# Two transformer blocks on one core: a token norm fed by a one-hot product, an earlier begin of a scan's operands, and q/k row sums in four row groups

## The chip, the cores and the metric

The kernel runs on one core of a Trainium2 chip. The metric is the device time in microseconds (us) of one execution, as the median of several runs. TensorE multiplies matrices, VectorE (DVE) and ScalarE (ACT) work on elements, GpSimd (POOL) builds masks and does some products, SyncE (SP) issues most of the transfers. Each engine runs its own list of instructions in order, and waits on semaphores for the others.

## The reference, cut to what matters

Two blocks follow one another on the same 1024 tokens of 1024 features. Three places of them matter here. The first is the norm of q and k in the first block's attention, over 64 features for each of 4 heads and 2 halves:

```python
q = rms_norm(q, g_q) * (HEAD_DK ** -0.5)
k = rms_norm(k, g_k)
```

The second is the seam of the blocks. 16 experts each pick 128 tokens (`idx`) and add their gated output to those rows; then the second block begins with a layer norm, whose result `h` feeds a projection and, times `DEEPNORM_ALPHA`, a residual:

```python
return jax.vmap(lambda ib, yb: jnp.zeros((S, D), yb.dtype).at[ib.reshape(-1)].add(yb.reshape(-1, D)))(idx, y)
...
h = layer_norm(x, ln_emb_g, ln_emb_b)
proj = jnp.einsum('bld,de->ble', h, w_in[i])
...
out = jnp.einsum('ble,ed->bld', mix, w_out[i]) + b_out[i]
h = layer_norm(DEEPNORM_ALPHA * h + out, ln1_g[i], ln1_b[i])
```

The third is the chunked scan of the second block: 8 chunks of 128 tokens by 2 groups of heads, which makes 16 steps. Each needs the decays `exp(segment sums)`, the inputs `x * dt`, and the state that the steps before have built.

## The kernel before

The program is seven blocks, one after the other, with a barrier between them. Inside a block the order on every engine is written by hand. Names used below: `Q` is PSUM, eight banks of 512 columns; `arena` is SBUF, cut into tiles of 1024 columns (`tiles(n)`); `W` is a ring of three slots for weight units of 2 MB, which SP refills as soon as the last reader of a slot is done; `hT_high` and `hT_low` are the two parts into which a float32 operand is split for three fast products. A plain float32 product shows in the trace as two records for one instruction, and is said below to be one float32 product.

**The q/k stage** (290.4 to 343.9 us of the trace). ScalarE squares the eight tiles of q and k. TensorE sums them over 64 features: `sums(g)` multiplies each by an 8-column mask into rows 0 to 7 (q) or 64 to 71 (k) of two PSUM banks. ScalarE takes the root (`root`), VectorE the reciprocal (`invert`) of these 8 rows by 1024 columns, `high_rows` and `low_rows` split them, and `spread` multiplies them back to 128 rows, for VectorE to scale q and k (`norm`, 8 of them). Between these, TensorE forms six vectors from weight units (`mod_product`, line 327; `next_vector(i)` is the row product of vector i and then the product of unit i + 1), VectorE adds their biases (`added`) and copies the far parts of the attention bias (lines 1064 and 1065).

**The token norm** (1250.2 to 1308.4 us). When the last expert's product is done, VectorE scales it (`outputs`) into `y_e`, GpSimd scatters it with add onto the tokens in DRAM (`scatter`), SP loads eight tiles of 128 tokens (`xt`), and VectorE normalizes each with two `bn_stats`, an aggregate, a reciprocal and two passes over 1024 columns (lines 2128 and 2130). TensorE turns each tile (8 transposes, line 1938), ScalarE and VectorE split the result (`emb_T`, `low_part`). From the fifth tile on, TensorE puts 12 products of the projection behind each tile. At the end it turns the small vectors (line 1951).

**The scan's begin** (from 1776 us). SP loads the segment sums of each step by broadcast (`send_sums`) into one of three places, `i % 3`, and the x inputs in four pieces (`send_xs`). ScalarE makes the decays (`decays`) and copies B out of PSUM (`read_turned`), VectorE makes `x * dt` (`inputs`) and the masked B C product (`chunk_cb`), GpSimd multiplies the decays by it. TensorE's `chunk(c)` needs both inputs of the chunk before.

## Time and profile before

| | |
|---|---|
| median of 3 runs (lowest, highest) | 2180.46 us (2178.20, 2182.43) |
| the profiled execution: time, span of its trace | 2185.76 us, 2184.0 us |
| mean granted TensorE clock, as a share of 2.4 GHz | 0.966 |
| TensorE busy | 2071.8 us, 95% of the span |
| VectorE busy | 1684.9 us, 77% |
| ScalarE busy | 1066.9 us, 49% |
| GpSimd busy | 215.8 us, 10% |

All times inside the kernel are positions in the one profiled execution, counted from its first instruction. Busy shares are means over stages with different limits, so each stage is read by itself. "Granted clock" 1.00 is TensorE's upper level (2.4 GHz), 0.50 its lower one (1.2 GHz). TensorE counts as busy from its first record to its last in a run of them, also at the lower level.

### The profile page before, as it was taken

How to read it: one execution, taken by the hardware profiler on the slowest of the kernel's cores; microseconds unless marked ns; L12 is line 12 of the kernel's file. 1: busy time of each engine (PE TensorE's matmuls, PEld its weight loads, DVE VectorE, ACT ScalarE, POOL GpSimd, SP SyncE). 2: the span in 40 equal slices, each digit the busy share in tenths (PEclk: the TensorE clock that was granted, in tenths of full speed). 3: DMA queues.
4: the chain of work that ended last, by engine and by line, in shares of the span. 5: the costliest groups of instructions: out<-in, count | busy, mean ns of one | idle time of the engine just before them, and what ended most of it. 6: DMA issues, size and time to landing. Idle time of an engine off the chain costs nothing. (4 is left out here: it accounts for less than half of the span.)

```text
span 2184.0 us, 24904 instructions
## 1 busy us (share of the span) xinstructions
PE 2071.8 (95%) x9840; PEld 1603.5 (73%) x9840; DVE 1684.9 (77%) x1714; ACT 1066.9 (49%) x1217; POOL 215.8 (10%) x168
## 2 busy tenths in 40 slices
PE   6999998999997999999999859999999998999998
PEld 4767844777865788888888647888888874588876
DVE  5575157895557899999999777999999977864776
ACT  4488134894235677777777522112222167523043
POOL 0200010001000011110110100000000013234040
PEclk9999997999988999999999969999999999899999
DMA  8311171003368999999999741111222245333121
GB/s 304 92 39 39 39 261 43 1 1 90 130 264 338 348 382 400 395 391 400 393 401 392 236 164 42 49 68 40 76 78 97 96 142 187 141 140 116 39 78 58
DMA packets 131071, 381.71 MB, mean 175 GB/s; under 512 B 9580, under 2 KB 22156, under 8 KB 130977
## 3 DMA queue, kind: packets, MB, share of 16 engines
q1 hardware_dynamic: 117184, 340.41, 40.9%
q0 software_dynamic: 7568, 23.09, 4.3%
q10 hardware_dynamic: 6224, 16.93, 1.9%
q8 instruction: 63, 1.03, 0.2%
q14 instruction: 32, 0.25, 0.0%
HBM read 337.28 MB, written 43.06 MB: 174 GB/s over the span
## 5 line engine op out<-in xcount | busy, mean ns | idle before, releaser
L2473 DVE SCALAR_TENSOR_TENSOR arena<-arena,vecs 128x1023 f32<-128x1023 f32 (+14 forms) x240 | 304.4, 1268 | 7.1
L2049 DVE TENSOR_TENSOR w_low<-W,w_high 128x2048 fp32r<-128x2048 f32 x96 | 216.9, 2286 | 34.2 <-ACT w_high L1970 34.2
L2049 DVE TENSOR_TENSOR w_low<-arena,w_high 128x2048 fp32r<-128x2048 f32 x96 | 218.4, 2289 | 19.3 <-ACT w_high L1970 19.3
L1822 PE MATMUL Q<-hT_high,w_high 128*128 128x512 f32 (+1 forms) x736 | 230.0, 392 | 1.3 <-PEq L1842 1.3
L1822 PE MATMUL Q<-hT_low,w_high 128*128 128x512 f32 (+1 forms) x720 | 225.0, 390 | 0.0
L1970 ACT ACTIVATE w_high<-arena 128x2048 fp32r<-128x2048 f32 x96 | 184.2, 1919 | 74.1 <-PE Q L1888 74.1
L1822 PE MATMUL Q<-hT_high,ring_low 128*128 128x512 f32 x704 | 219.9, 390 | 0.0
L1970 ACT ACTIVATE w_high<-W 128x2048 fp32r<-128x2048 f32 x96 | 184.0, 1919 | 69.3 <-PE Q L1888 65.6
L1835 ACT ACTIVATE w_high<-W 128x1024 fp32r<-128x1024 f32 x44 | 46.6, 1059 | 256.1 <-PE Q L1822 243.0
L1888 PE MATMUL Q<-w_high,x_high 128*128 128x512 f32 x512 | 160.9, 396 | 2.4 <-DVE x_low L2052 2.4
L1822 PEld LDWEIGHTS Q<-hT_high,w_high 128*128 128x128 f32 (+1 forms) x736 | 135.4, 184 | 33.2 <-issue 1.8
L1888 PE MATMUL Q<-w_low,x_high 128*128 128x512 f32 x512 | 158.9, 392 | 0.0
L1888 PE MATMUL Q<-w_high,x_low 128*128 128x512 f32 x512 | 158.7, 391 | 0.0
L1822 PEld LDWEIGHTS Q<-hT_low,w_high 128*128 128x128 f32 (+1 forms) x720 | 134.1, 186 | 29.6
L1822 PEld LDWEIGHTS Q<-hT_high,ring_low 128*128 128x128 f32 x704 | 132.6, 188 | 27.8
L1888 PEld LDWEIGHTS Q<-w_low,x_high 128*128 128x128 f32 x512 | 97.1, 190 | 20.5
L1888 PEld LDWEIGHTS Q<-w_high,x_high 128*128 128x128 f32 x512 | 95.9, 190 | 21.7 <-DVE x_low L2052 2.8
L1888 PEld LDWEIGHTS Q<-w_high,x_low 128*128 128x128 f32 x512 | 96.8, 189 | 20.4
L468 PE MATMUL Q<-h_high,in_high 128*128 128x512 f32 x254 | 100.7, 396 | 0.0
L469 PE MATMUL Q<-h_high,ring_low 128*128 128x512 f32 x254 | 99.4, 391 | 0.0
L470 PE MATMUL Q<-h_low,in_high 128*128 128x512 f32 x254 | 99.1, 390 | 0.0
L1173 DVE CUSTOM_DVE_ANT_0 arena<-Q,arena 128x1024 f32<-128x1024 f32 x64 | 76.0, 1223 | 22.5 <-PE Q L1128 22.4
(466 smaller groups left out, 4139.9 us busy)
## 6 DMA issues: line engine op xcount, KB each, us to landing
arena<-in_w_dram SPq DMA_DIRECT2D x48, 2048.0 KB, 12.3
W<-in_w_dram SPq DMA_DIRECT2D x48, 2048.0 KB, 13.2
W<-in_w_mod_dram SPq DMA_DIRECT2D x12, 2048.0 KB, 13.3
W<-in_w_in_dram SPq DMA_DIRECT2D x12, 2048.0 KB, 9.2
W<-in_w_out_dram SPq DMA_DIRECT2D x6, 2048.0 KB, 10.8
spill<-arena ACTq DMA_DIRECT2D x24, 512.0 KB, 2.6
W<-in_w_in_dram SPq DMA_DIRECT2D x8, 1024.0 KB, 8.8
arena<-spill SPq DMA_DIRECT2D x3, 2048.0 KB, 10.8
```

Source lines behind the costliest of these rows:

```text
L468: nc.tensor.matmul(bank, w_high, h_high, start=first, stop=False)
L469: nc.tensor.matmul(bank, w_low, h_high, start=False, stop=False)
L470: return nc.tensor.matmul(bank, w_high, h_low, start=False, stop=last)
L1173: nc.vector.tensor_tensor_reduce(out=score[i % 3][j], in0=bank2(j), in1=bias, scale=1.0, scalar=3.0e38, op0=ALU.add, op1=ALU.min, accum_ou ...
L1822: ins = nc.tensor.matmul(Q[rows, 2 * pair_of(n) + half, :], w[:, k], x[:, k, HALF * half:HALF * half + HALF], start=k == 0 and w is high a ...
L1835: nc.scalar.activation(high, src, ACT.Copy).then_inc(split_high, 1)
L1888: ins = nc.tensor.matmul(Q[:, bank + n, :], x[:, kx], w[:, k, HALF * n:HALF * n + HALF], start=kx == 0 and x is high and w is wh, stop=kx ...
L1970: nc.scalar.activation(split_of(r, j)[0][:], chunk_src(r, j), ACT.Copy).then_inc(high_ready, 1)
L2049: nc.vector.tensor_tensor(wl[:], chunk_src(r, j), wh[:].bitcast(F32), ALU.subtract).then_inc(low_v, 1)
L2473: ins = nc.vector.scalar_tensor_tensor(conf[:, i, j:], u[:, 0:S - j], w, conf[:, i, j:], ALU.mult, ALU.add)
```

## The change

Three edits that don't touch one another.

1. **q/k norm.** The mask `qk_sum` repeats its 8 columns to 32, and `sums` computes four blocks of 32 output rows, one for each quarter of the 1024 columns, all in one bank. The rows are now 128 by 256 instead of 8 by 1024 for root, reciprocal and split; a column of 0 and 1 (`lower`, `sign`) makes half of each group of rows carry the low part, and VectorE writes them with four instructions of 32 rows into `qk_parts`. The mask for `spread` is the transpose of `qk_sum`, made on TensorE. The eight spreads and norms move between the other work.
2. **Token norm.** SP loads the first four tiles before the last expert's sums are scattered. TensorE adds them: the tile times the identity, plus a one-hot matrix (`picked`, made on VectorE from `idx`) times `y_e`, both float32. Statistics are read from PSUM. ScalarE does the first pass (scale and shift), VectorE one pass for the gain. The bias `ln_emb_b` is added on TensorE behind each transpose as a one-row product, and for the residual in a row `row_sum` = ALPHA * ln_emb_b + b_out. `turn_vecs` moves ahead of the last tiles' products.
3. **The scan's begin.** The sums' places change to 0, 1, 0, 1, 2, 0, 1, ... (`sums_place`), so that step 2's are asked for in step 3's old place. `read_turned(1)` moves into `decays(2)`, and `inputs(1)` moves ahead of the last three products of `conf` (k = 5, 6, 7).

The diff, cut to its core:

```diff
-        qk_sum = tiles(5)[:, 0:HEADS * VECS].rearrange("p (b r) -> p b r", b=HEADS)
...
+        QUARTER, REPEAT = S // 4, P // VECS
+        qk_sum = tiles(4)[:, 0:HALF].rearrange("p (b r) -> p b r", b=HEADS)
...
+        qk_high = rounded("qk_high", 2, [P, 4, QUARTER])
...
-                        for half in range(2):
-                            ins = nc.tensor.matmul(Q[rows_of(g), sum_bank[g] + half, :], qk_sum[:, b],
-                                                   tiles(n % 2)[:, HALF * half:HALF * half + HALF],
+                        for q in range(4):
+                            ins = nc.tensor.matmul(Q[32 * q:32 * q + 32, sum_bank[g], 0:QUARTER], qk_sum[:, b, 0:32],
+                                                   tiles(n % 2)[:, QUARTER * q:QUARTER * q + QUARTER],
                                                    start=b == 0, stop=b == HEADS - 1)
...
                             next_vector(2 * g + b // 2)
+                        if g and b:
+                            spread(b - 1)
                         if n == 1:
                             near()
...
+                    if g:
+                        spread(HEADS - 1)
+                def spread(n):
+                    g, b = divmod(n, HEADS)
+                    pe.wait_ge(mask_ready, 1)
                     pe.wait_ge(parts_low, g + 1)
...
+                    if n >= 2:
+                        pe.wait_ge(qk_normed, n - 1)
+                    for half in range(2):
+                        ins = nc.tensor.matmul(Q[:, 6 * (n % 2) + half, :], qk_spread[:, b],
+                                               qk_parts[:, HALF * half:HALF * half + HALF], start=True, stop=True)
+                    ins.then_inc(spread_mm, 1)
...
                 def invert(g):
                     dve.wait_ge(root_q, g + 1)
-                    nc.vector.reciprocal(qk_rows[rows_of(g)], qk_rows[rows_of(g)]).then_inc(rows_inv, 1)
+                    nc.vector.reciprocal(qk_rows[:, g], qk_rows[:, g]).then_inc(rows_inv, 1)
+                    dve.wait_ge(rows_inv, g + 1)
+                    nc.vector.tensor_scalar_mul(qk_lower, qk_rows[:, g], lower).then_inc(qk_lower_ready, 1)
                 def low_rows(g):
                     dve.wait_ge(parts_high, g + 1)
-                    nc.vector.tensor_tensor(qk_parts[rest_of(g)], qk_rows[rows_of(g)],
-                                            qk_parts[rows_of(g)].bitcast(F32), ALU.subtract).then_inc(parts_low, 1)
+                    dve.wait_ge(qk_lower_ready, g + 1)
+                    if g:
+                        dve.wait_ge(spread_mm, HEADS)
...
+                    for q in range(4):
+                        at = slice(32 * q, 32 * q + 32)
+                        ins = nc.vector.scalar_tensor_tensor(
+                            qk_parts[at, QUARTER * q:QUARTER * q + QUARTER], qk_high[at, 2 + g].bitcast(F32),
+                            sign[at], qk_lower[at], ALU.mult, ALU.add)
+                    ins.then_inc(parts_low, 1)
...
-                for h in range(HEADS):
+                def far(h):
...
+                far(0)
+                for n in range(HEADS - 1):
+                    norm(n)
+                    far(n + 1)
                 added(3)
+                norm(HEADS - 1)
                 invert(1)
+                low_rows(1)
                 added(4)
-                norm(0)
-                low_rows(1)
-                for n in range(1, HEADS):
-                    norm(n)
+                norm(HEADS)
+                norm(HEADS + 1)
                 added(5)
-                for n in range(HEADS, 2 * HEADS):
-                    norm(n)
+                norm(HEADS + 2)
+                norm(HEADS + 3)
...
+        sums_place = [i if i < 2 else (i - 2) % 3 for i in range(STEPS)]
+        def sums_of(i):
+            return cs_bc[sums_place[i]]
...
         def send_sums(sync, i):
...
-            sync.dma_start(cs_bc[i % 3], rows.broadcast_to((P, HPG * P))).then_inc(cs_in[i % 3], 16)
+            sync.dma_start(sums_of(i), rows.broadcast_to((P, HPG * P))).then_inc(sums_in(i)[0], 16)
...
+                sync.wait_ge(*low_level(E, 3))
+                sync.dma_start(b_row, A["ln_emb_b_2"].rearrange("(o n) -> o n", o=1)).then_inc(rows_b_in, 16)
+                sync.dma_start(bo_row, A["b_out_2"][0].rearrange("(o n) -> o n", o=1)).then_inc(rows_b_in, 16)
+                sync.wait_ge(h_tr, E)
+                sync.wait_ge(y_added, 16 * (E - 1))
+                for t in range(PICKED):
+                    sync.dma_start(xt[t], tokens_acc[P * t:P * t + P]).then_inc(xt_in[t], 16)
+                sync.wait_ge(row_sum_ready, 1)
+                sync.dma_start(row_sum, b_sum).then_inc(row_stored, 16)
+                sync.wait_ge(emb_sum, PICKED)
                 sync.wait_ge(y_added, 16 * E)
-                for t in range(NT):
+                for t in range(PICKED, NT):
                     sync.dma_start(xt[t], tokens_acc[P * t:P * t + P]).then_inc(xt_in[t], 16)
                 for t in range(NT):
...
+                def token_sum(t):
+                    pe.wait_ge(xt_in[t], 16)
+                    if t >= 2:
+                        pe.wait_ge(emb_scaled, t - 1)
+                    for n in range(2):
+                        nc.tensor.matmul(Q[:, 4 + 2 * (t % 2) + n, :], ident[:], xt[t][:, HALF * n:HALF * n + HALF],
+                                         start=True, stop=False)
+                    if t == 0:
+                        pe.wait_ge(picked_ready, 1)
+                        pe.wait_ge(y_ready, E)
+                    for n in range(2):
+                        ins = nc.tensor.matmul(Q[:, 4 + 2 * (t % 2) + n, :], picked[:, t],
+                                               y_e[:, HALF * n:HALF * n + HALF], start=False, stop=True)
+                    ins.then_inc(emb_sum, 1)
+                def turn_vecs():
+                    pe.wait_ge(small2_in, 16 * (4 + NT + 8))
...
+                    ins.then_inc(vec_tr, 1)
+                pe.wait_ge(y_ready, E - 1)
+                token_sum(0)
+                pe.wait_ge(rows_b_in, 32)
                 for t in range(NT):
+                    if t + 1 < PICKED:
+                        token_sum(t + 1)
                     pe.wait_ge(emb_ready, t + 1)
                     if t >= 2:
                         pe.wait_ge(emb_T_low, t - 1)
                     for k in range(KD):
...
+                        turned_k = Q[:, 2 * (t % 2) + k // 4, P * (k % 4):P * (k % 4) + P]
+                        nc.tensor.matmul(turned_k, xt[t][:, P * k:P * k + P], ident[:], start=True, stop=False,
+                                         is_transpose=True)
+                        ins = nc.tensor.matmul(turned_k, b_row[:, P * k:P * k + P], ones[0:1, :],
+                                               start=False, stop=True)
                     ins.then_inc(emb_tr, 1)
+                    if t == NT - 2:
+                        turn_vecs()
...
-                root(0)
-                for t in range(NT):
-                    if t + 1 < NT:
-                        root(t + 1)
+                def emb_high(t):
                     act.wait_ge(emb_tr, t + 1)
...
+                root(0)
+                for t in range(NT):
+                    act.wait_ge(emb_shift, t + 1)
+                    nc.scalar.activation(xt[t], bank2(2 + t % 2) if t < PICKED else xt[t], ACT.Identity,
+                                         bias=shift_col[t % 2], scale=rstd[:, t:t + 1]).then_inc(emb_scaled, 1)
+                    if t:
+                        emb_high(t - 1)
+                    if t + 1 < NT:
+                        root(t + 1)
+                emb_high(NT - 1)
...
+                v_link(nc.vector.tensor_tensor_scan(count, ones[:], ones[:], 0.0, ALU.mult, ALU.add))
...
+                for t in range(PICKED):
+                    v_link(nc.vector.tensor_scalar_add(slot_at[:, 1 + t:2 + t], slot_at[:, 0:1], 1.0 - P * t))
+                    ins = nc.vector.tensor_tensor(picked[:, t], count, slot_at[:, 1 + t:2 + t].broadcast_to((P, P)),
+                                                  ALU.is_equal)
+                ins.then_inc(picked_ready, 1)
+                dve.wait_ge(rows_b_in, 32)
+                nc.vector.scalar_tensor_tensor(b_sum, b_row, ALPHA, bo_row, ALU.mult, ALU.add).then_inc(row_sum_ready, 1)
                 outputs(E - 1, pair=0)
                 low_part2(dve, 1)
                 stats(0)
...
                 for t in range(NT):
                     dve.wait_ge(emb_var, t + 1)
+                    dve.wait_ge(emb_root, t + 1)
+                    v_link(nc.vector.reciprocal(rstd[:, t:t + 1], rstd[:, t:t + 1]))
+                    nc.vector.tensor_scalar(shift_col[t % 2], emb_mv[t % 2][:, 0:1], rstd[:, t:t + 1], -1.0,
+                                            ALU.mult, ALU.mult).then_inc(emb_shift, 1)
                     if t + 1 < NT:
                         stats(t + 1)
-                    dve.wait_ge(emb_root, t + 1)
-                    v_link(nc.vector.reciprocal(rstd[:, t:t + 1], rstd[:, t:t + 1]))
-                    v_link(nc.vector.scalar_tensor_tensor(xt[t], xt[t], emb_mv[t % 2][:, 0:1], emb_g,
-                                                          ALU.subtract, ALU.mult))
-                    nc.vector.scalar_tensor_tensor(xt[t], xt[t], rstd[:, t:t + 1], emb_b,
-                                                   ALU.mult, ALU.add).then_inc(emb_ready, 1)
+                    dve.wait_ge(emb_scaled, t + 1)
+                    nc.vector.tensor_tensor(xt[t], xt[t], emb_g, ALU.mult).then_inc(emb_ready, 1)
...
+                    if isinstance(e, int) and e == E - 1:
+                        for t in range(PICKED):
+                            pool.wait_ge(xt_in[t], 16)
...
                 send_sums(sync, 1)
-                sums_behind(3)
+                sums_behind(2)
                 sync.wait_ge(in2_mm, len(order))
                 send_xs(1)
-                send_sums(sync, 2)
+                sums_behind(3)
                 send_xs(2)
...
+                    if i == 2:
+                        act.wait_ge(cg_used, 6)
+                        read_turned(1)
...
+                    if k == 5:
+                        inputs(1)
```

The q/k stage on VectorE, before (rows of one engine's program in order: line, operation, output<-inputs, shape, what it waits for; L1022 is an addition of a vector's bias, L1043 a norm, L1064 and L1065 the far copies):

```order
L1034 RECIPROCAL arena<-arena 8x1024 [waits root_q]
L1022 TENSOR_TENSOR arena<-Q,arena 128x512 [waits row_mm]
L1038 TENSOR_TENSOR qk_parts<-arena,qk_parts 8x1024 [waits parts_high]
L1064 COPY arena<-arena 128x768 [waits near_ready]
L1065 COPY arena<-arena 128x768
...
L1034 RECIPROCAL arena<-arena 8x1024 [waits root_q]
...
L1043 SCALAR_TENSOR_TENSOR arena<-arena,small,Q 128x1024 [waits spread_mm]
L1038 TENSOR_TENSOR qk_parts<-arena,qk_parts 8x1024 [waits parts_high]
L1043 SCALAR_TENSOR_TENSOR arena<-arena,small,Q 128x1024 [waits spread_mm] x3
...
L1043 SCALAR_TENSOR_TENSOR arena<-arena,small,Q 128x1024 [waits spread_mm] x4
```

And of the changed kernel, where L1058 is the norm, L1051 the split and L1082 and L1083 the far copies:

```order
L1038 RECIPROCAL arena<-arena 128x256 [waits root_q]
L1040 TENSOR_SCALAR arena<-arena 128x256 [waits rows_inv]
L1051 SCALAR_TENSOR_TENSOR qk_parts<-qk_high,arena 32x256 [waits qk_lower_ready,masks,parts_high,sign_ready]
L1051 SCALAR_TENSOR_TENSOR qk_parts<-qk_high,arena 32x256 x3
...
L1058 SCALAR_TENSOR_TENSOR arena<-arena,small,Q 128x1024 [waits spread_mm]
L1082 COPY arena<-arena 128x768
L1083 COPY arena<-arena 128x768
...
L1038 RECIPROCAL arena<-arena 128x256 [waits root_q]
L1040 TENSOR_SCALAR arena<-arena 128x256 [waits rows_inv]
L1051 SCALAR_TENSOR_TENSOR qk_parts<-qk_high,arena 32x256 [waits spread_mm,qk_lower_ready,parts_high]
...
L1058 SCALAR_TENSOR_TENSOR arena<-arena,small,Q 128x1024 [waits spread_mm] x2
```

Four norms now stand between and behind the far copies, ahead of the second reciprocal; the other four stay last.

The seam of the blocks on TensorE, before: the last expert's products (L1888), the transposes of the tiles (L1938), the projection's first products (L1822).

```order
L1888 MATMUL Q<-w_low_5255,h_high 128x512 x2
L1888 MATMUL Q<-w_high_5251,h_low 128x512 x2
L1938 MATMUL Q<-ident,arena 128x128 x40
L1822 MATMUL Q<-hT_high,w_high_5258 128x512
L1822 MATMUL Q<-hT_low,w_high_5258 128x512
L1822 MATMUL Q<-hT_high,ring_low 128x512
```

And after, where L1989 adds a tile by the identity, L1995 the one-hot product, L2018 is a transpose and L2020 the bias behind it:

```order
L1989 MATMUL Q<-arena,ident 128x512 x2
L1995 MATMUL Q<-arena 128x512 x2
L1989 MATMUL Q<-arena,ident 128x512 x2
L1995 MATMUL Q<-arena 128x512 x2
L2018 MATMUL Q<-ident,arena 128x128
L2020 MATMUL Q<-ones,arena 128x128
...
L1989 MATMUL Q<-arena,ident 128x512 x2
L1995 MATMUL Q<-arena 128x512 x2
L2018 MATMUL Q<-ident,arena 128x128
L2020 MATMUL Q<-ones,arena 128x128
```

Each tile has 16 instructions where it had 8, and the sums of tiles 2 and 3 stand behind the transposes of tiles 0 and 1.

The scan's begin on ScalarE, before: the decays of step 2 (L2365, L2370, L2373), the copy of the turned B (L2379), the first split of the scan's output (L2383).

```order
L2365 ACTIVATE W<-W,keep 128x128 [waits cs_in2]
L2365 ACTIVATE W<-W,keep 128x128 x7
L2370 ACT_TABLE_LOAD
L2370 ACTIVATE small<-W 128x8
L2373 ACTIVATE W<-W 128x1024 [waits relu_ready]
L2379 ACTIVATE arena<-Q 128x256 [waits chunk_mm]
L2383 ACTIVATE conf_high<-arena 128x8x128 [waits cg_used]
```

And after:

```order
L2467 ACTIVATE W<-W,keep 128x128 [waits cs_in0]
L2467 ACTIVATE W<-W,keep 128x128 x7
L2484 ACTIVATE arena<-Q 128x256 [waits chunk_mm,cg_used]
L2475 ACT_TABLE_LOAD
L2475 ACTIVATE small<-W 128x8
L2478 ACTIVATE W<-W 128x1024 [waits relu_ready]
L2488 ACTIVATE conf_high<-arena 128x8x128 [waits cg_used]
```

The copy now stands inside the decays of step 2, between their subtractions and their exponentials, and waits there for TensorE's `chunk(1)`.

## Rows read from the trace of the kernel before

**Rows 1.** windows: span us; busy PE, PEld, DVE, ACT, POOL; clock; DMA share, GB/s
```profile
290.40:343.90 53.50, 46.07 (x166) 12.98 (x166) 39.62 (x42) 21.05 (x24) 9.15 (x17) 0.84 0.84 310
1250.20:1308.40 58.20, 26.29 (x124) 21.15 (x124) 44.60 (x60) 12.20 (x18) 7.75 (x10) 0.65 0.45 162
```

**Rows 2.** waits of TensorE: total us, times, longest
```profile
PE Q L1938 <- DVE arena L2130: 30.7, 6, 17.9
```

**Rows 3.** timeline of VectorE, q/k stage: start us, us, engine, line
```profile
309.73 6.53 DVE L1034 RECIPROCAL arena<-arena 8x1024 f32<-8x1024 f32 x1
...
318.69 0.56 DVE L1064 COPY arena<-arena 128x768 f32<-128x768 f32 x1
...
338.64 5.06 DVE L1043 SCALAR_TENSOR_TENSOR arena<-arena,small,Q 128x1024 f32<-128x1024 f32 x4 [0.46 <-PE Q L940]
```

**Rows 4.** timeline of TensorE, q/k stage
```profile
317.10 3.60 PE L923 MATMUL Q<-arena 128*8 128x512 f32 x8
...
321.68 1.92 PE L327 MATMUL Q<-W,keep 128*32 128x512 f32 x16
```

**Rows 5.** DMA issued in 298 to 300: KB each, us to landing
```profile
W<-in_w_mod_dram SPq DMA_DIRECT2D x1, 2048.0 KB, 19.5
```

**Rows 6.** timelines of TensorE and VectorE at the convolution's mean and root
```profile
1755.37 3.66 PE L2315 MATMUL Q<-arena,ones 128*32 128x256 f32 x64
...
1776.68 1.75 DVE L2636 RECIPROCAL arena<-arena 128x256 f32<-128x256 f32 x1 [1.75 <-ACT arena L2440]
```

**Rows 7.** timeline of VectorE, token norm
```profile
1262.17 1.29 DVE L2042 BATCH_NORM_STATS2 small<-arena 128x6 f32<-128x512 f32 x2 [9.58 <-DMA arena<-tokens_acc]
```

**Rows 8.** timeline of TensorE, token norm
```profile
1237.32 0.73 PE L1888 MATMUL Q<-w_high,h_high 128*128 128x512 f32 x2 [3.30 <-DVE h_low L2052]
...
1277.61 1.97 PE L1938 MATMUL Q<-ident,arena 128*128 128x128 f32 x8 [3.27 <-DVE arena L2130]
...
1298.56 1.09 PE L1938 MATMUL Q<-ident,arena 128*128 128x128 f32 x8 [0.63 <-DVE arena L2130]
...
1302.40 1.09 PE L1938 MATMUL Q<-ident,arena 128*128 128x128 f32 x8
...
1306.19 0.94 PE L1951 MATMUL Q<-ident,arena 42*128 42x42 f32 x12
```

**Rows 9.** timeline of TensorE, one chunk of the scan
```profile
1821.27 0.61 PE L2256 MATMUL Q<-arena 128*128 128x128 f32 x4
1821.72 1.02 PE L2277 MATMUL Q<-W,arena 128*128 128x512 f32 x2
```

**Rows 10.** queue of SP; DMA issued in 1236 to 1237.3, and in 1258.5 to 1259.3
```profile
1233.93 2.84 SPq L258 DMA_DIRECT2D W<-in_w_in_dram  x1
...
W<-in_w_in_dram SPq DMA_DIRECT2D x1, 2048.0 KB, 16.8
...
tokens_acc<-arena,idx POOLq DMA_INDIRECT x1, 8.6
...
arena<-tokens_acc SPq DMA_DIRECT2D x2, 512.0 KB, 4.0
```

**Rows 11.** timelines at the scan's start, three engines
```profile
1807.43 1.09 PE L2251 MATMUL Q<-ident,arena 128*128 128x128 f32 x8 [4.12 <-DVE arena L2527]
...
1808.46 2.44 ACT L2365 ACTIVATE W<-W,keep 128x128 f32<-128x128 f32 x8 [4.84 <-DMA W<-cs_rows]
...
1814.29 2.36 POOL L2227 TENSOR_TENSOR W<-W 128x1024 f32<-128x1024 f32 x1 [10.45 <-DVE W L2553]
```

**Rows 12.** DMA issued in 1796.85 to 1801.7
```profile
W<-cs_rows SPq DMA_DIRECT2D x1, 512.0 KB, 7.3
arena<-spill SPq DMA_DIRECT2D x1, 512.0 KB, 4.6
```

**Rows 13.** windows of two stretches of the token norm, columns as in rows 1
```profile
1238.30:1242.00 3.70, 3.70 (x11) 2.86 (x10) 2.30 (x2) 0.00 (x0) 0.00 (x0) 0.54 1.14 341
1268.00:1288.00 20.00, 7.88 (x32) 6.28 (x32) 19.45 (x28) 4.83 (x8) 0.00 (x0) 0.50 0.38 153
```

130 lines of the change are left out of this document (68 added, 62 removed).

## The prediction, made before the changed kernel ran

> **What bounds the kernel now.** I read the page first: TensorE is busy for 95% of the span, so an edit can only pay where TensorE waits or does less. Then I read each of the three stages by its window and the timelines of its engines.
>
> In the q/k stage TensorE is busy 46.07 of 53.5 us, VectorE 39.62 [rows 1]. At its end VectorE sets the pace: two reciprocals of 8 rows take 6.53 us each, and four norms close the stage at 343.7 [rows 3].
>
> In the token norm TensorE is busy 26.29 of 58.2 us and VectorE 44.60 [rows 1]. TensorE waited 30.7 us in six waits for the second pass over a tile (line 2130), once 17.9 us [rows 2]. The first tile's statistics began at 1262.17, after 9.58 us of waiting for a transfer [rows 7]; from then on VectorE needed 3.27 + 1.97 = 5.24 us a tile [rows 8]. TensorE was through at 1306.19 + 0.94 = 1307.1, and ran at its lower level meanwhile: granted clock 0.50 from 1268 to 1288 [rows 13].
>
> At the scan's start ScalarE waited 4.84 us for the sums of step 2, GpSimd 10.45 for its product, TensorE 4.12 for `inputs` [rows 11]. The arrival of the sums at 1808.46 sets the begin.
>
> The profiled execution took 2185.76 us (span 2184.0), 5.3 more than the median of 2180.46. The sum below is a difference against the profiled one, and is taken off the median. About 0.2%, 4.4 us, is what a measurement of this kernel can tell from no change.
>
> **A: q/k norm, -8 us (-12 to -4).** The convolution's norm has the new shapes: 32 float32 products of 256 columns into 32 rows took 3.66 us, 0.114 each, and a reciprocal of 128 by 256 took 1.75 [rows 6]. Four float32 products of 512 columns (eight records) take 3.60 us [rows 4], so a tile's sums go from 1.8 to 0.46 us. The two reciprocals lose 2 x (6.53 - 1.75) = 9.6 us.
>
> Not all of it arrives, since `next_vector(3)` holds the rest. It ends with the product of a weight unit that is issued near 299.1 and lands 19.5 us later, at 318.6 [rows 5], while the DMA engines are busy for 84% of the stage [rows 1]; the change brings it no earlier. The product takes 1.92 us [rows 4] and `spread(2)` 0.6, so VectorE gets its input at 321.1. Behind it stand six norms at 1.26, two far copies, 0.56 each with some overlap, 0.95 together, three additions of 512 columns, estimated at half a norm, 0.63, and a reciprocal of 1.75 [rows 3, 6]: 7.6 + 0.95 + 1.9 + 1.75 = 12.2. Not in the trace are a scalar product of 128 by 256 and four splits of 32 by 256. By elements a row they are a quarter of a norm, 0.32 each, which makes 1.6; by the far copy's pace a little less; with a fixed part 2.0. I take 2.0. So the stage ends at 321.1 + 14.2 = 335.3, 8.4 earlier, and I take 8, since TensorE may spread at its lower level. If the unit doesn't hold, the full 9.6 and some of the sums arrive (-12); if each step behind it waits on TensorE at that level, half of it (-4).
>
> **B: token norm, +8 us (-1 to +18).** The last weight unit is issued at 1233.9 and lands 16.8 later, at 1250.7 [rows 10]; the first tile, issued while the weights still run, follows at 1252 (an estimate; issued only then it would land 4.0 us behind them [rows 10], which costs 2.7 more). The scatter's 8.6 us [rows 10] and the wait of 9.58 [rows 7] are no longer in its way. The sum of a tile is four float32 products of 512 columns, 3.6 us [rows 4]. VectorE's norm needs the second tile's statistics ahead of the first tile's gain pass, so two sums come first: 1252 + 7.2 = 1259.2. Statistics take 1.29 [rows 7] and the pass a norm's 1.27 [rows 3]; with the small steps between, 3.8: the first tile is ready at 1263.0. Before, TensorE waited for it 17.9 us from 1250.1, to 1268.0 [rows 1, 2]. That is 5 us won.
>
> Then it is lost. The sums of tiles 2 and 3 stand behind the transposes of tiles 0 and 1. So tile 1's gain pass waits for: transposes of tile 0, sum of tile 2, statistics of tile 2. Eight transposes at the upper level take 0.85 (1.09 with their end) [rows 8], and the bias adds eight float32 products of 128 columns: four records, two products, took 0.45, so 0.22 each [rows 9], 1.7 in all. With the sum: 0.85 + 1.7 + 3.6 = 6.2. But TensorE restarts after 3 us of waiting, and when it had waited 3.30 us for VectorE up to 1237.32 [rows 8], it ran at granted clock 0.54 from 1238.3 to 1242 [rows 13]; 3.7 us at about half are 1.7 lost: 7.9. Statistics, pass and signals add 3.0. The period is 10.9 instead of 5.24, twice: tile 2 is ready at 1284.8. Tiles 4 to 7 are only asked for when the fourth sum is done, near 1281.8, and land 4.0 later [rows 10], in time. VectorE now needs 5.24 - 1.27 = 4.0 a tile, so tile 4 is ready at 1292.8. Before it was at 1277.61 + 2 x 5.24 = 1288.1, and TensorE's end came 19.0 later; a tile with its 12 projection products took 1302.40 - 1298.56 = 3.84 there [rows 8]. The bias adds 4 x 1.7 = 6.8 and the wait of 0.63 goes: 25.2. So 1318.0 against 1307.1, +10.9, less about 1.3 because `vecs` is copied ahead of the end: +9.6. If every burst ran at the upper level it would be 3.4 less, and 2.5 less again in tile 4: +3.7. I take +8, nearer the first, as the restarts look like that of [rows 13]. If a bias product cost only a transpose's 0.11 as well, 5 us less: -1. If TensorE stayed at its lower level throughout: +18, below. What is moved besides (one-hot masks, `b_sum`, GpSimd's wait for the four tiles) lies in time in which VectorE and GpSimd waited: VectorE's 9.58 [rows 7]. Without that cover the masks would cost about 3 us.
>
> The Trainium skill says in "TensorE: Matmul & The Clock Gate", Part 4, that a transpose in transpose mode doesn't count as work for the clock gate, so that the full clock doesn't engage. The trace agrees: transposes alone, 0.50 [rows 13]. By that rule the restarts here, which begin with transposes, are long, and the sum would be nearer +18 than +4.
>
> **C: the scan's begin, -3.2 us (-4.5 to -1.5).** The sums of step 2 take the place in the queue that step 3's had, at 1796.9, and need 7.3 us [rows 12]: 1804.2 instead of 1808.46. ScalarE's subtractions take 2.44 [rows 11] and end at 1806.6. Now `read_turned(1)` waits for `chunk(1)`. Its inputs wait for an x piece issued at about 1801.4, 4.6 us [rows 12], so it starts at 1806.05 instead of 1807.43 [rows 11], and takes 2.1. The copy, the table load and the exponentials follow to 1811.0. From then on the order is as before, where GpSimd's product began at 1814.29 [rows 11]: 3.3 earlier. Afterwards TensorE sets the pace. If the sums share the DMA engines with more than they did, 1.5 remain.
>
> **Sum:** -8 + 8 - 3.2 = -3.2 us. 2180.46 - 3.2 = 2177.3.
>
> **The rivals.**
>
> *Slower: the lower level throughout the token norm.* If TensorE never gets to its upper level in the serial part, transposes and bias take 5.1 and a sum 7.2, and the period is 15.3: 2 x 4.4 = 8.8 more than in my sum, so B is +18 and the time 2187.5. For it speaks 0.50 over 20 us of transposes [rows 13]; against it, that the whole stage had 0.65 [rows 1], so that the clock did come back once TensorE had more to do than transposes, and the sums are long products. It decides from B above 15.6, a period of 14. Chance 0.16.
>
> *The token norm costs little.* With bursts at the upper level, or bias products that overlap the transposes, B is between -1 and +4, say +2: 2173.3. For it: the waits of 3 us are just shorter than the 3.27 at which TensorE stayed low. Against it: the one restart that the trace shows. Chance 0.25.
>
> *The weight unit lands later.* The next unit is asked for earlier, because its slot is free earlier. If the two share the DMA engines, A gives -5.5 instead of -8: 2179.8, no change. Against it: the units landed one after another. The rule in the Trainium skill, "DMA: Bandwidth & Descriptors", on queues and rings, that a ring's descriptors are consumed in order, says the same; I know of no row against it. Chance 0.13.
>
> **Chances.** The forecast 0.42 (its own range 2174 to 2182), the three rivals 0.16, 0.25 and 0.13, the rest 0.04. Faster by over 0.2% (under 2176.1): the second rival and a third of the forecast, 0.40. Slower by over 0.2% (over 2184.8): most of the first, and the rest, 0.17. Within 0.2%: 0.43. The range is 2169.5 to 2187.5, which leaves the outermost of the bounds of A and B out, 0.2 in all.
>
> **What would show it.** Right: reciprocals of 1.75 us, norms ending near 335; first transposes near 1263, then two periods of 11 us with waits of 3 us on the gain pass; the four last tiles 5.5 us apart, TensorE through near 1318; the sums of step 2 at 1804 and GpSimd's product near 1811. Wrong: a third vector later than 321; a period near 9 or 15; first tiles that land behind 1253; a stage in which nothing is edited and the time moves all the same.

## The result: 48 us slower, and where they are

The changed kernel took 2229.45 us (median; 2228.12 to 2232.92) where the kernel before took 2181.44 in the same comparison: a ratio of 1.0216, 95% interval 1.0201 to 1.0231. The forecast was 2177.3, the range ended at 2187.5. The profiled execution has a span of 2226.4 us, 42.4 more than before.

The windows of the changed kernel, columns as in [rows 1]: the q/k stage, the whole token norm, and a part of the latter.

```profile
293.20:340.20 47.00, 37.39 (x202) 11.88 (x202) 32.73 (x51) 18.40 (x26) 8.08 (x12) 0.85 0.96 353
1244.20:1356.40 112.20, 101.74 (x284) 61.04 (x284) 36.66 (x61) 22.19 (x26) 7.02 (x10) 0.67 0.23 80
1290.00:1308.00 18.00, 17.91 (x48) 10.86 (x48) 7.95 (x15) 3.65 (x4) 0.00 (x0) 0.50 0.62 234
```

The q/k stage lasts 47.0 us instead of 53.5 [rows 1], as wanted. The token norm lasts 112.2 instead of 58.2: **+54 us**. TensorE was busy 26.29 us of it before [rows 1]; now it is busy 101.74. The third row is the most telling: from 1290 to 1308 TensorE is busy 17.91 of 18 us, without waiting, and its granted clock is 0.50 all the time.

TensorE's waits in the token norm, and the groups of its instructions there (busy us, mean ns of one, idle before). `1*128` are the rows and columns of the array that a product fills with weights, here one row:

```profile
PE Q L2018 <- DVE arena L2228: 8.2, 3, 2.7
```
```profile
L2020 PE MATMUL Q<-ones,arena 1*128 1x128 f32 x128 | 44.4, 441 | 0.0
L2018 PE MATMUL Q<-ident,arena 128*128 128x128 f32 x64 | 27.0, 422 | 8.2 <-DVE arena L2228 8.2
```

The wait for VectorE fell from 30.7 us [rows 2] to 8.2, just what an early first tile and a shorter pass should do. But it was replaced by work: 44.4 us of one-row bias products (line 2020) and 27.0 us of transposes (line 2018). Neighbouring records overlap by their modelled ends; from the first to the last of each tile's it is 62 us for the eight tiles. The timeline of TensorE shows how:

```profile
1256.07 0.48 PE L2018 MATMUL Q<-ident,arena 128*128 128x128 f32 x1 [2.72 <-DVE arena L2228]
1256.48 0.79 PE L2020 MATMUL Q<-ones,arena 1*128 1x128 f32 x2
1257.20 0.47 PE L2018 MATMUL Q<-ident,arena 128*128 128x128 f32 x1
...
1273.67 0.33 PE L2018 MATMUL Q<-ident,arena 128*128 128x128 f32 x1 [2.72 <-DVE arena L2228]
1273.93 0.48 PE L2020 MATMUL Q<-ones,arena 1*128 1x128 f32 x2
1274.34 0.33 PE L2018 MATMUL Q<-ident,arena 128*128 128x128 f32 x1
...
1276.38 0.48 PE L2018 MATMUL Q<-ident,arena 128*128 128x128 f32 x1
1276.78 0.79 PE L2020 MATMUL Q<-ones,arena 1*128 1x128 f32 x2
1277.50 0.47 PE L2018 MATMUL Q<-ident,arena 128*128 128x128 f32 x1
...
1290.09 0.48 PE L2018 MATMUL Q<-ident,arena 128*128 128x128 f32 x1 [2.72 <-DVE arena L2228]
```

The first transposes start at 1256.07; everything ahead of the stage is 6 us earlier, so this is 1262 on the clock of before, and the forecast said 1263.0. Up to here it went as predicted. Then a transpose and its bias product take 1257.20 - 1256.07 = 1.13 us at the lower level, and 1274.34 - 1273.67 = 0.67 at the upper. The forecast had 0.11 + 0.22 = 0.33 at the upper. And at 1276.4, in the middle of unbroken work, the clock falls back: from there a pair takes 1.12 us again. The periods are 1273.67 - 1256.07 = 17.6 and 16.4 us, against 10.9 in the forecast and 5.24 before.

The q/k stage on VectorE, and the third vector's product on TensorE:

```profile
310.30 1.74 DVE L1038 RECIPROCAL arena<-arena 128x256 f32<-128x256 f32 x1
312.08 0.35 DVE L1040 TENSOR_SCALAR arena<-arena 128x256 f32<-128x256 f32 x1
312.65 1.95 DVE L1051 SCALAR_TENSOR_TENSOR qk_parts<-qk_high,arena 32x256 fp32r<-32x256 f32 x4 [0.21 <-ACT qk_high L989]
...
337.67 2.46 DVE L1058 SCALAR_TENSOR_TENSOR arena<-arena,small,Q 128x1024 f32<-128x1024 f32 x2
```
```profile
322.53 1.92 PE L328 MATMUL Q<-W,keep 128*32 128x512 f32 x16 [2.71 <-DMA W<-in_w_mod_dram]
```

A reciprocal takes 1.74 us instead of 6.53 [rows 3]. The scalar product and the four splits take 2.5 us together, from 312.08 to 314.60 (2.0 were forecast for all five). The norms end at 340.1 instead of 343.7, though the stage began 2.8 us later here. The product behind the weight unit started at 322.53 after 2.71 us of waiting for it.

The scan's begin on TensorE and GpSimd:

```profile
1854.31 1.06 PE L2353 MATMUL Q<-ident,arena 128*128 128x128 f32 x8 [3.02 <-DMA arena<-spill]
...
1845.98 2.39 POOL L2329 TENSOR_TENSOR W<-W 128x1024 f32<-128x1024 f32 x1 [1.09 <-ACT W L2478]
...
1859.13 2.36 POOL L2329 TENSOR_TENSOR W<-W 128x1024 f32<-128x1024 f32 x1 [7.37 <-ACT W L2478]
```

From GpSimd's first product (1797.99 before) to its third it is 13.15 us, where it was 16.3 [rows 11]: 3.15 less, with 3.2 forecast.

### The profile page after: what moved, and what is told of

The parts are those of the page before. It is cut to its first block and busy times, and to the rows that moved or that the text cites. A ratio compares the mean times of both kernels' runs of the same rounds, so it can differ in the third digit from the quotient of the medians.

```text
span 2226.4 us, 25340 instructions
## 1 busy us (share of the span) xinstructions
PE 2133.9 (96%) x10036; PEld 1640.1 (74%) x10036; DVE 1674.0 (75%) x1734; ACT 1074.0 (48%) x1227; POOL 215.1 (10%) x163
## 5 line engine op out<-in xcount | busy, mean ns | idle before, releaser
L1938 PE MATMUL Q<-w_high,x_high 128*128 128x512 f32 x512 | 160.4, 395 | 2.4 <-DVE x_low L2140 2.4
L1938 PE MATMUL Q<-w_low,x_high 128*128 128x512 f32 x512 | 158.6, 391 | 0.0
L1938 PE MATMUL Q<-w_high,x_low 128*128 128x512 f32 x512 | 158.4, 391 | 0.0
L1938 PEld LDWEIGHTS Q<-w_low,x_high 128*128 128x128 f32 x512 | 96.8, 189 | 20.4
L1938 PEld LDWEIGHTS Q<-w_high,x_high 128*128 128x128 f32 x512 | 95.7, 190 | 21.7 <-DVE x_low L2140 2.8
L1938 PEld LDWEIGHTS Q<-w_high,x_low 128*128 128x128 f32 x512 | 96.7, 189 | 20.3
## 6 DMA issues: line engine op xcount, KB each, us to landing
W<-in_w_mod_dram SPq DMA_DIRECT2D x12, 2048.0 KB, 13.8
```

Of the source, the lines that this page charges most:

```text
L1938: ins = nc.tensor.matmul(Q[:, bank + n, :], x[:, kx], w[:, k, HALF * n:HALF * n + HALF], start=kx == 0 and x is high and w is wh, stop=kx ...
```

## The experiments

A table worked out from the traces helps to read them. For each kernel it has the length of three stretches, in us: q/k (from the stage's first product on TensorE to VectorE's first instruction of the attention), token norm (from TensorE's restart after the last wait of 3.3 us in the experts to VectorE's first run of the convolution's taps), scan's begin (from GpSimd's first product to its third). Each row is read from one profiled execution, and the time is the median of all (the kernel before, measured again beside each group of runs, had medians of 2181.4 to 2184.2). The profiled one lay 7.0 us above the median in e5 and 4.7 in e7, so a difference of a microsecond or two between two rows shows nothing by itself.

| kernel | q/k | token norm | scan's begin | time, median |
|---|---|---|---|---|
| before | 57.3 | 85.6 | 16.3 | 2182 |
| changed | 50.4 | 139.6 | 13.2 | 2229.5 |
| e1: q/k and scan edits alone | 48.4 | 87.5 | 14.3 | 2174.0 |
| e2: no bias products | 48.2 | 81.6 | 14.6 | 2173.3 |
| e3: transposes, then bias products | 50.2 | 108.0 | 14.9 | 2199.0 |
| e4: two bias products of 8 rows | 50.3 | 108.1 | 13.4 | 2199.2 |
| e5: q/k edit alone | 51.9 | 85.6 | 17.3 | 2177.0 |
| e6: scan edit alone | 57.3 | 87.2 | 16.0 | 2182.3 |
| e7: bias on VectorE | 51.3 | 95.5 | 13.8 | 2183.9 |
| e8: e7, sums further ahead | 51.8 | 84.6 | 15.3 | 2174.6 |
| e9: pairs, each to another place | 52.0 | 135.9 | 13.7 | 2224.2 |
| e10: e3 with 128-row bias products | 51.6 | 99.1 | 14.2 | 2187.1 |

### e1: the token norm of before

```diff
@@ against the changed kernel
-                token_sum(0)
-                for t in range(NT):
-                    if t + 1 < PICKED:
-                        token_sum(t + 1)
...
-                        ins = nc.tensor.matmul(turned_k, b_row[:, P * k:P * k + P], ones[0:1, :],
-                                               start=False, stop=True)
```

(and with it all of edit 2, as in the diff above the prediction).

> The q/k edit and the scan edit alone; the token norm is that of the kernel before. Theory one (the token norm is the whole loss: in the trace of the changed kernel it costs 54 us, from the stage's begin to the next product of the projection): about 54 us less than the changed kernel, 2170 to 2176, so 5 to 11 us under the kernel before, with 7 from q/k (its stage ended 4.1 us earlier though it began 2.8 later) and 3 from the scan. Rival (the loss isn't in the token norm alone, the other edits share in it): not under 2181.

Measured: 2174.0 us, ratio to before 0.9954 (0.9940 to 0.9969). The token norm is the whole loss, 55 us; the other two edits together win about 8 to 10 (interval 7 to 13).

### e2: no bias products

```diff
-                        nc.tensor.matmul(turned_k, xt[t][:, P * k:P * k + P], ident[:], start=True, stop=False,
-                                         is_transpose=True)
-                        ins = nc.tensor.matmul(turned_k, b_row[:, P * k:P * k + P], ones[0:1, :],
-                                               start=False, stop=True)
+                        ins = nc.tensor.matmul(turned_k, xt[t][:, P * k:P * k + P], ident[:], start=True, stop=True,
+                                               is_transpose=True)
```

> The changed kernel without the one-row bias products behind the transposes (ln_emb_b is thereby missing in h and its projection; the residual keeps it). Theory one: a pair of transpose and bias product took 1.13 us at TensorE's lower level and 0.67 at its upper in the changed kernel, where a transpose alone took 0.25 and 0.11 before; 64 pairs thus cost about 50 us, and they keep the clock low. Without them the period of the serial part falls from 17 to 8 to 12 us, and the time to 2170 to 2182. Rival (the sums by identity and one-hot, behind the transposes in TensorE's order, are the loss): the period stays above 14 us and the time above 2200.

Measured: 2173.3 us, 0.9955 (0.9941 to 0.9969). TensorE's timeline:

```profile
1260.35 1.09 PE L2018 MATMUL Q<-ident,arena 128*128 128x128 f32 x8 [2.72 <-DVE arena L2226]
1261.28 1.88 PE L1989 MATMUL Q<-arena,ident 128*128 128x512 f32 x4
1263.00 1.88 PE L1995 MATMUL Q<-arena 128*128 128x512 f32 x4
1267.60 1.09 PE L2018 MATMUL Q<-ident,arena 128*128 128x128 f32 x8 [2.72 <-DVE arena L2226]
```

The period is 7.25 us, the wait for the gain pass is the same 2.72, and these tiles run at the upper level, eight transposes in 0.93. The 64 bias products cost 139.6 - 81.6 = 58 us. The sums, the rival, cost nothing net, and win nothing either: with them and no bias the kernel is as fast as e1, though it leaves out the bias, which e1 adds.

### e3: the same products, grouped

```diff
                     for k in range(KD):
                         turned_k = Q[:, 2 * (t % 2) + k // 4, P * (k % 4):P * (k % 4) + P]
-                        nc.tensor.matmul(turned_k, xt[t][:, P * k:P * k + P], ident[:], start=True, stop=False,
+                        nc.tensor.matmul(turned_k, xt[t][:, P * k:P * k + P], ident[:], start=k % 4 == 0, stop=False,
                                          is_transpose=True)
+                    for k in range(KD):
+                        turned_k = Q[:, 2 * (t % 2) + k // 4, P * (k % 4):P * (k % 4) + P]
                         ins = nc.tensor.matmul(turned_k, b_row[:, P * k:P * k + P], ones[0:1, :],
-                                               start=False, stop=True)
+                                               start=False, stop=k % 4 == 3)
```

> The same products in another order: the eight transposes of a tile first, then its eight one-row bias products. Theory one, first form (it is the alternation that costs: each product of a pair waits for the other, at the same place in PSUM and with another mode): a tile takes 8 x 0.25 + 8 x 0.43 = 5.4 us at the lower level instead of 9.0, and 2.6 instead of 5.4 at the upper; the time falls by 25 to 35 us, to about 2200. Second form (a one-row float32 product costs what it costs, in any order): the time stays at 2225 to 2231 and a bias product still stands 0.4 us (upper) or 0.7 us (lower) from the next.

Measured: 2199.0 us, 1.0069 (1.0052 to 1.0085): 30.5 us less than the changed kernel, for the order and the start and stop flags that it needs. Against e9 below, which has the same flags and alternates, it is 25.2 less.

```profile
1256.01 1.96 PE L2018 MATMUL Q<-ident,arena 128*128 128x128 f32 x8 [2.72 <-DVE arena L2230]
1257.90 3.78 PE L2022 MATMUL Q<-ones,arena 1*128 1x128 f32 x16
...
1284.35 1.10 PE L2018 MATMUL Q<-ident,arena 128*128 128x128 f32 x8 [2.72 <-DVE arena L2230]
1285.37 2.52 PE L2022 MATMUL Q<-ones,arena 1*128 1x128 f32 x16
```

Eight transposes take 1.89 us and eight bias products 3.71 at the lower level, 1.02 and 2.0 to 2.5 at the upper (the group at 1285.37 ends at the lower one). So a pair is worth 0.70 us at the lower level in this order, and cost 1.13 alternating; at the upper level 0.25 for the product and 0.13 for the transpose, against 0.67. That a product costs 0.25 is what [rows 9] said (0.22). What the forecast left out is the price of going over from a transpose to a one-row product and back: 0.67 - 0.38 = 0.29 us a pair at the upper level and 1.13 - 0.70 = 0.43 at the lower. For 64 pairs that makes 19 to 28 of the 30 us.

### e4: two products of 8 rows instead of eight of one

```diff
-                        ins = nc.tensor.matmul(turned_k, b_row[:, P * k:P * k + P], ones[0:1, :],
-                                               start=False, stop=True)
+                    for n in range(2):
+                        ins = nc.tensor.matmul(
+                            Q[:, 2 * (t % 2) + n, :], b_rows[:],
+                            ident[0:KD, 4 * n:4 * n + 4].rearrange("p (k o) -> p k o", o=1).broadcast_to((KD, 4, P)),
+                            start=False, stop=True)
```

> The bias of four transposes is added by one product of 512 columns: weights are the bias as 8 rows of 128, the moving side is an identity of 8 with each column repeated 128 times; two such float32 products a tile in place of eight one-row ones. Theory one in both forms: two products of 0.9 us (upper level) or 1.8 (lower) and eight transposes at their own price, 2.7 or 5.6 us a tile instead of 5.4 or 9.0; period 11 to 15 us, time 2190 to 2205. Rival (the sums and the low clock are the loss, not the number of bias products): above 2215.

Measured: 2199.2 us, 1.0069 (1.0045 to 1.0092), as e3. Its bias products at the lower level:

```profile
1260.72 3.78 PE L2023 MATMUL Q<-ident,arena 8*128 8x512 f32 x4
```

The same 3.7 us as sixteen records of one row: here the columns are paid for, neither the rows nor the number of instructions.

### e9: alternating, but never at the place just written

```diff
-                    for k in range(KD):
+                    for n in range(KD + 1):
...
+                        if n < KD:
+                            k = n
...
+                            nc.tensor.matmul(turned_k, xt[t][:, P * k:P * k + P], ident[:], start=k % 4 == 0,
+                                             stop=False, is_transpose=True)
+                        if n:
+                            k = n - 1
...
+                            ins = nc.tensor.matmul(turned_k, b_row[:, P * k:P * k + P], ones[0:1, :],
+                                                   start=False, stop=k % 4 == 3)
```

> Transposes and one-row bias products alternate as in the changed kernel, but the bias product behind the transpose of block k is that of block k - 1, so that it adds to other columns than those just written. If a pair costs 0.67 us (upper level) because the product waits for the transpose's result at the same place, the time falls to that of the grouped order, 2199. If it costs that because TensorE changes between a transpose and a float32 product, whatever the place, it stays at 2225 to 2231 with 1.13 us from pair to pair at the lower level.

Measured: 2224.2 us, 1.0185 (1.0168 to 1.0202), just under the 2225 to 2231 expected.

```profile
1273.40 0.79 PE L2025 MATMUL Q<-ones,arena 1*128 1x128 f32 x2
1274.12 0.48 PE L2020 MATMUL Q<-ident,arena 128*128 128x128 f32 x1
1274.53 0.79 PE L2025 MATMUL Q<-ones,arena 1*128 1x128 f32 x2
```

From product to product it is 1274.53 - 1273.40 = 1.13 us at the lower level, as in the changed kernel. So it is not a wait for the result at the same place. Two things still change with every instruction of a pair: the kind (transpose or float32 product) and the number of rows of the array that are used (128 or 1). Groups at the upper level in three traces tell them apart. First e10 (below), where transposes are followed by products of 128 rows, then e3, where one-row products follow, then e2, where transposes of 128 rows are followed by transposes of 42:

```profile
1296.10 1.03 PE L2021 MATMUL Q<-ident,arena 128*128 128x128 f32 x8
1296.97 1.95 PE L2025 MATMUL Q<-arena 128*128 128x128 f32 x16
```
```profile
1304.39 1.03 PE L2018 MATMUL Q<-ident,arena 128*128 128x128 f32 x8
1305.36 2.05 PE L2022 MATMUL Q<-ones,arena 1*128 1x128 f32 x16
```
```profile
1291.94 1.04 PE L2018 MATMUL Q<-ident,arena 128*128 128x128 f32 x8
1292.91 0.94 PE L2003 MATMUL Q<-ident,arena 42*128 42x42 f32 x12
```

From the first of eight transposes to what follows it is 0.87, 0.97 and 0.97 us, where a transpose takes 0.11. Another kind with the same 128 rows costs nothing extra (e10); other rows cost 0.1 us, also between transpose and transpose (e2). So, as far as these traces show, the extra time of a pair goes with the number of rows, not with the kind. Single transposes alternating with products of 128 rows were not run. The 5 us below the changed kernel are two changes fewer at each tile's ends and less at the lower level; how they divide was not measured.

### e10: bias products of 128 rows

```diff
+                sync.dma_start(emb_b, bc_row(A["ln_emb_b_2"], D)).then_inc(rows_b_in, 16)
...
+                nc.vector.tensor_scalar_mul(part, ones[:], 1.0 / P)
...
-                        ins = nc.tensor.matmul(turned_k, b_row[:, P * k:P * k + P], ones[0:1, :],
+                        ins = nc.tensor.matmul(turned_k, emb_b[:, P * k:P * k + P], part[:],
```

(against e3).

> The grouped order, but each bias product has 128 rows instead of one: the bias broadcast to 128 rows times a tile of 1/128; the same number of products and columns, one more transfer of 512 KB. If TensorE's clock falls back because one-row products leave the array nearly empty, the granted clock between the first and the last transposes rises from 0.65 to 0.9 or more, a tile costs 3.0 instead of 5.7 us and the time falls by 10 to 18 us to 2181 to 2189. If transposes alone, or the waits of 2.7 us, keep it low, the time stays at 2196 to 2202.

Measured: 2187.1 us, 1.0009 (0.9995 to 1.0024): 11.9 us less than e3, with the same number of records and columns. First the same stretch in e3, then in e10:

```profile
1256.00:1285.00 29.00, 23.55 (x70) 15.35 (x71) 7.56 (x14) 5.04 (x6) 1.92 (x4) 0.65 0.10 33
```
```profile
1256.00:1285.00 29.00, 21.06 (x101) 16.54 (x102) 13.34 (x25) 7.77 (x11) 1.49 (x4) 0.82 0.23 75
```

The granted clock of the stretch is 0.82 instead of 0.65 (0.9 was expected: a tile still starts at the lower level after its wait). And inside e10:

```profile
1281.35 2.43 PE L2025 MATMUL Q<-arena 128*128 128x128 f32 x16
1283.62 1.04 PE L2021 MATMUL Q<-ident,arena 128*128 128x128 f32 x8
1284.49 1.95 PE L2025 MATMUL Q<-arena 128*128 128x128 f32 x16
```

The products bring the clock up: eight transposes from 1283.62 take 0.87 us, and eight products 1.9. In the changed kernel 18 us of unbroken transposes and one-row products didn't. Of what the bias costs in e3 (26 us over e2), 9 to 12 us are gone in e10 (by the table and by the medians). About 2 of them are the changes of rows (0.1 us before each group and 0.1 in it), the rest is the lower level. What e10 still takes over e2, 17.5 us in the table and 13.8 by the medians, are mostly the products themselves, 8 x 2.0 to 2.7.

### e5 and e6: the other edits alone

```diff
@@ e5: against the kernel before, edit 1 alone
-                    nc.vector.reciprocal(qk_rows[rows_of(g)], qk_rows[rows_of(g)]).then_inc(rows_inv, 1)
+                    nc.vector.reciprocal(qk_rows[:, g], qk_rows[:, g]).then_inc(rows_inv, 1)
...
@@ e6: against the kernel before, edit 3 alone
-            sync.dma_start(cs_bc[i % 3], rows.broadcast_to((P, HPG * P))).then_inc(cs_in[i % 3], 16)
+            sync.dma_start(sums_of(i), rows.broadcast_to((P, HPG * P))).then_inc(sums_in(i)[0], 16)
...
```

> The q/k edit alone. From the two edits together (8.4 us under the kernel before) and the stage's own shift in the changed kernel: the norms end 4 to 8 us earlier, whole time 5 to 7 us under the kernel before. Rival (the late weight unit, which landed at 322.5 in the changed kernel instead of 318.6, is an effect of the edit and eats most of it): 2 to 4 us.

Measured: 2177.0 us, 0.9979 (0.9968 to 0.9990), 2 to 7 us less than before, which doesn't decide between the 5 to 7 expected and the rival's 2 to 4. In five kernels with the edit (e1, e5, e7, e8, e10) TensorE waited 2.4 to 3.2 us for the same weight unit and went on between 319.1 and 322.2; it holds the stage as argued.

> The scan edit alone. Its begin came 3.15 us earlier in the changed kernel: time 3 us under the kernel before, 2 to 4. Rival (the 2.4 us that the changed kernel gained besides, between the scan's first step and its end, belong to the edit as well): 5 us or more.

Measured: 2182.3 us, 0.9997 (0.9988 to 1.0007): nothing, where 3 us were expected. Its scan started so:

```profile
1806.81 1.94 PE L2263 MATMUL Q<-ident,arena 128*128 128x128 f32 x8 [4.39 <-DMA arena<-spill]
```

The x piece came 4.39 us after TensorE was ready and 6.1 us after its issue, where the changed kernel waited 3.02 us and its piece took 4.7; and the transposes behind it took 1.94 us instead of 1.06, at the lower level. The table shows the spread: 13.2 to 15.3 us in the nine other kernels with the edit, 16.3 and 17.3 in two without. The edit wins 1 to 3 us up to the third product; alone it is below what the comparison can show. And not all of this lasts. GpSimd's fifth product began at 1823.96 before (the first at 1797.99) and at 1870.16 in the changed kernel (the first at 1845.98). That is 26.0 us and 24.2, so 1.8 of the 3.15 us are left. In e6 it is 25.7; in the ten kernels with the edit 23.1 to 26.6, in the two without 26.0 and 29.0.

### e7 and e8: a token norm with the sums that doesn't lose

e7 has e2's transposes, and adds the bias on VectorE; e8 besides has the sums of tile t + 2 ahead of the transposes of tile t.

```diff
-                    nc.vector.tensor_tensor(xt[t], xt[t], emb_g, ALU.mult).then_inc(emb_ready, 1)
+                    v_link(nc.vector.tensor_tensor(xt[t], xt[t], emb_g, ALU.mult))
+                    nc.vector.tensor_tensor(xt[t], xt[t], emb_b, ALU.add).then_inc(emb_ready, 1)
...
-                for dst, v in ((b_out, row_sum[0]), (ln1_g, A["ln1_g_2"][0])):
+                for dst, v in ((b_out, A["b_out_2"][0]), (ln1_g, A["ln1_g_2"][0])):
@@ e8
                 token_sum(0)
+                token_sum(1)
...
-                    if t + 1 < PICKED:
-                        token_sum(t + 1)
+                    if t + 2 < PICKED:
+                        token_sum(t + 2)
```

> All three edits, with the one-hot sums, but the bias added by VectorE in a second pass over each tile (as the kernel before did) and not on TensorE. Without any bias the kernel took 2173.3. A pass of 1.2 us comes into the period of the serial part, three times, and into the tiles 4 and on, where VectorE needs 5.2 us again: 4 to 7 us more than without, 2177 to 2180. If VectorE's pass is hidden behind TensorE's sums: 2173 to 2175, as with the token norm of before.

> The same with the sum of tile t + 2, not t + 1, ahead of the transposes of tile t, so that the sums stand no longer between one tile's transposes and the next one's statistics. If the serial chain (transposes, sum, statistics, pass: 7.25 us a period without bias) is where the gain of the early first tile went, the period becomes VectorE's 5.2 and the time falls by 2 x 3 = 6 us against the kernel with the bias on VectorE in the old order, to 2168 to 2174. Rival (the tiles 4 to 7 set the pace, since they are loaded only after the fourth sum): no change.

Measured: e7 2183.9 us, 1.0009 (0.9997 to 1.0021); e8 2174.6, 0.9959 (0.9946 to 0.9973). First e7, then e8:

```profile
1263.18 1.97 PE L2020 MATMUL Q<-ident,arena 128*128 128x128 f32 x8 [3.98 <-DVE arena L2229]
...
1268.35 1.95 PE L1997 MATMUL Q<-arena 128*128 128x512 f32 x4
1274.28 1.10 PE L2020 MATMUL Q<-ident,arena 128*128 128x128 f32 x8 [3.98 <-DVE arena L2229]
```
```profile
1261.39 1.09 PE L2021 MATMUL Q<-ident,arena 128*128 128x128 f32 x8
...
1266.55 1.04 PE L2021 MATMUL Q<-ident,arena 128*128 128x128 f32 x8
1270.76 1.97 PE L2021 MATMUL Q<-ident,arena 128*128 128x128 f32 x8 [3.17 <-DVE arena L2230]
1275.99 1.97 PE L2021 MATMUL Q<-ident,arena 128*128 128x128 f32 x8 [3.27 <-DVE arena L2230]
```

e7 missed its 2177 to 2180. The wait is 3.98 us now, behind it transposes and sum begin at the lower level (1263.18 to 1268.35: 5.2 us for what took 2.7 in e2), and the period is 11.1 us, where 7.25 + 1.2 = 8.5 would have made the forecast. In e8 no sum stands in the chain; the third, fourth and fifth tile come 5.23 us apart, VectorE's pace, and 9.3 us are won against e7, more than the 6 expected; the time is just above the 2168 to 2174 expected, since e7 was slower than thought. e8 beats both kernels, but is no faster than e1 (2174.0): its first transposes come at 1261.39, since three sums stand ahead of them and the first runs at the lower level. What skipping the scatter wins, the sums about cost.

## Why the prediction was wrong, by its steps

**A: right in mechanism, a little high in size.** Forecast -8 (-12 to -4). The stage was 5.3 to 9.1 us shorter in the ten kernels with the edit, the whole time 5.2 (2 to 7) alone. The reciprocals were as argued, and the weight unit holds the stage; it landed 0.5 to 4 us later than the 318.6 of the forecast, at 322.5 in the changed kernel, whose stage also began 2.8 us later. The third rival, a later unit, had -5.5, which fits the measured time at least as well. Whether two units shared the DMA engines, as it says, was not looked at.

**B: wrong.** Forecast +8 (-1 to +18), measured +54. The first tile came as forecast. The step that failed is "the bias adds eight float32 products of 128 columns ... 0.22 each, 1.7 in all". The price of one product was right (0.25), and the sum of the parts was not the price of the pair: alternating with transposes, a pair costs 0.67 or 1.13 us, not 0.33. The order listing showed the alternation; every row that I priced from was a run of one kind. Yet the trace of the kernel before has an alternation too, in the scan behind [rows 9], at the upper level:

```profile
1802.21 1.09 PE L2292 MATMUL Q<-W 128*64 128x128 f32 x16
...
1821.05 0.38 PE L2254 MATMUL Q<-ident,arena 128*128 128x128 f32 x2
...
1823.15 0.33 PE L2288 MATMUL Q<-ident,W 128*128 128x128 f32 x1
1823.41 0.44 PE L2292 MATMUL Q<-W 128*64 128x128 f32 x4
1823.78 0.33 PE L2288 MATMUL Q<-ident,W 128*128 128x128 f32 x1
```

A transpose that fills 128 columns of the array and four records that fill 64 take 1823.78 - 1823.15 = 0.63 us. By themselves they are at most 0.11 + 1.09 / 4 = 0.38, so the way over and back costs at least 0.25 there. The two transposes at 1821.05 and the products of [rows 9] at 1821.27 fill the same part of the array; there 0.22 us pass, the price of two transposes, and the change costs nothing. So the trace of before held both a change that is free and one that is not, there by the number of columns, and [rows 9] was one of the free ones.

The second step that failed is that a restart costs 3.7 us at about half speed, then no more. It was read from experts' products of 128 rows and 512 columns [rows 13], and used for transposes and one-row products, which e10 and the window 1290 to 1308 show do not bring TensorE to its upper level. The first rival had the lower level throughout, and even so a period of 15.3 instead of 17.6 and 16.4, since its pairs were too cheap; and it charged the lower level only to the serial part. Most of the loss was behind it: from tile 2's transposes to the stage's end it was 1356.4 - 1290.1 = 66 us, against 33 forecast. There every tile had 9.0 us (lower) or 5.4 (upper) of pairs where before it had 1.97 or 1.09.

The rule cited there, in the Trainium skill's "TensorE: Matmul & The Clock Gate", Part 4, that transposes in transpose mode don't count as work for the clock, pointed this way: by it the sum was to be nearer +18. The runs agree with it as far as they go (0.50 over transposes alone, with waits between them [rows 13]), and add that one-row and 8-row products don't help either (e4, 1291.3 to 1302.0: transposes and 8-row products, busy 10.69 of 10.7 us at 0.50). I gave it too little weight: it was applied to the restart alone and not to the whole stretch.

**The upper bound** of B was no bound. It had "the lower level throughout" times the wrong price of a pair. For an order of operations that the rows in use don't show (two kinds alternating on one engine), the rest of the trace has to be searched for one, as above, or the range has to be wider.

**C: right up to GpSimd's third product, not behind it.** Forecast -3.2 (-4.5 to -1.5). At the third product it was -3.15 in the changed kernel, and -0.3 to -3.15 over the ten kernels with the edit. "From then on the order is as before" was true of the order and not of the time: by the fifth product 1.8 were left. Alone the edit made 0.

**The sum.** 42.4 us between the two spans: +54 in the token norm, -6 ahead of it, and -5.6 from the scan on. Of the last, 1.8 are what is left of the scan's begin. Most of the rest came in one later stretch of the same products. It took 28.1 us before (1878.3 to 1906.4) at a granted clock of 0.76, and 25.6 in the changed kernel (1924.5 to 1950.1) at 0.93. These 2.5 us belong to no edit that I could name.

## What to carry to other kernels

Price an added product in its place among its neighbours, not by itself: on TensorE, one-row products put between transposes of 128 rows cost 0.3 to 0.4 us a pair beyond their own time, and grouping them gave back 30 of 48 us without taking any work out. Look for such changes of rows or columns in the order listing. One-row products behind transposes also don't bring TensorE to its upper level, and a tile's pairs take 9.0 us instead of 5.4; look at the granted clock of a stretch in which it is busy without a break. And where a wait vanishes from the profile, look at what the busy time of the engine became: here 30.7 us of waiting turned into 75 us of work.

## What the runs showed of the hardware that was not expected

- A transpose and a one-row float32 product of 128 columns, alternating: 0.67 us a pair at the upper level and 1.13 at the lower, against 0.38 and 0.70 in two groups, where the product has one row; 1.13 also when it goes to other columns than those just written (e9). Groups show the extra time where the number of rows changes (0.1 us from transposes to one-row products in e3, and from 128-row to 42-row transposes in e2), and none where only the kind does (e10).
- 18 us of unbroken transposes and one-row products at granted clock 0.50; and a fall from the upper to the lower level at 1276.4 without a wait. Products with 128 rows in their place, as many and as long: 0.82 instead of 0.65 over 29 us (e10).
- Two products of 8 rows by 512 columns cost as much as eight of one row by 128 columns: 3.7 us at the lower level (e3, e4).
- After the same wait of 2.72 us TensorE restarted at the upper level in e2 and at the lower one in e3, with the same instructions before it, of which the first had run at the lower level in e2; the wait alone doesn't tell.
